# Sixteen weight blocks copied to a contiguous scratch tensor during the projection, and the scan's weight loads read from there

## The chip, the core and the metric

The kernel runs on one core of one Trainium2 chip. The metric is the device time of one execution in microseconds (us). Nothing runs beside it on the other cores. Five engines work in parallel, each through its own list of instructions, and meet at semaphores: PE multiplies matrices, ACT applies functions and copies, DVE and POOL do element-wise work, SP only issues transfers. ACT and POOL issue transfers too; those of SP appear in the profile as queue q1, those of ACT as q10, those of POOL as q0. The data move through 16 DMA engines, and the DMA share of a stretch is the mean busy share of these 16.

## The reference, cut to what matters

A layer over 2048 latent tokens with 256 context tokens in front. One input projection of the modulated, normalised tokens gives all branches; the columns of `in_w` are its outputs.

```
IN_SIZES = (M_WIDTH, M_WIDTH, M_WIDTH, M_WIDTH, M_WIDTH, N_GATE_COLS, P_WIDTH, P_WIDTH, N_BRANCH * D_MODEL)
names    = ('q',     'k',     'v',     'o',     'z_m',   'gates',     'p',     'z_p',   'g_branch')

parts_x = _split_proj((_rmsnorm(x, norm_w) * (1 + scale) + shift) @ in_w)
h_x     = _bi_mlstm(qx, kx, vx, lix, lfx, st_f, st_b)          # two scans over chunks of 128 tokens
y       = hn * sigmoid(parts['o']) * silu(parts['z_m'])        # then @ branch_m_w
y_p     = _pool_branch(parts_x, ...)                           # box means of p, times silu(z_p)
x       = x + gate * ((sigmoid(g_m) * y_m + sigmoid(g_p) * y_p) @ out_w)
return _rmsnorm(x, final_norm_w)
```

Here D_MODEL is 1024, there are 4 heads of 256, and `in_w` is 1024 rows by 8208 columns of float32. A row of it is thus 32,832 bytes long.

## The kernel before, in words

Everything is float32, multiplied as a high and a low part (three matmuls for each product), so every weight block is loaded raw, then split by ACT (`wh`) and DVE (`wl`). Four stages follow each other, each a block of its own at whose end all engines meet.

1. **Entry**, 0 to about 145 us: modulation, norms, and the transposed, split inputs `xlate`, `xtop`, `xctx` in on-chip memory.
2. **Projection**, about 145 to 908 us: the columns q, k, v and p with z_p ("s" in the code). The work is 32 units of 256 columns over 1024 tokens. A unit is seven block products M1, M6, M7, M5, M2, M4, M3 with sums of weight blocks and of results around them; an eighth product E belongs to the context tokens in eight of the units. That makes 232 positions, `POS`, and position p is about 3.3 us long. Every engine walks the same loop over p. ACT loads the next unit's raw weights (`raw_in`, in_w in pieces of 1 KB, or of 512 bytes for "s") when it splits M1. It splits three products ahead of PE. POOL makes the sums of weight blocks (`sums`, four for each unit) and the low parts of q and k (`low`). SP stores what is finished: q, k and v in transfers of 1 MB (`store_qk`, `store_v`), p and z_p in transfers of 256 KB. At the start of the second half of the tokens (from p = 113 on) seven blocks of inputs are rebuilt from a raw copy in HBM, `xr_d`, through a ring of eight slots called `stage` (`block_in`, L1058).
3. **Scan**, about 908 to 1940 us: PE interleaves the scan's steps with the projection's remaining columns: o, z, and the two gate parts g_m and g_p. Their weights are 16 blocks of 256 columns (`SCAN_COLS`, four for each of o, z, g_m, g_p). They are needed for both halves of the tokens, so 32 loads of 1 MB are made. ACT issues them (`pair`, L1772), one about every 31 us, into the buffer `wpair`, which is the same memory as `wraw`: the profile calls it `wraw`. The order is trip by trip: trip 0 takes the first block of o, z, g_m and g_p, trip 1 the second of each, and so on to trip 3; trips 4 to 7 repeat this for the other half of the tokens. The first of the 32 loads is issued at the end of stage 2 (L1144), the other 31 in stage 3. A load fetches, for each of the 128 partitions, eight pieces of 256 columns, which lie 128 rows of `in_w` apart.
   The scan's own data come through SP in many small transfers (`v_t`, `q_t`, `k_t`, `s_t`, `hother`), and its results go out the same way.
4. **Exit**, about 1940 to 2487 us: branch projections, merge, output projection, final norm.

The semaphores that the change touches: `prod_done` counts PE's products in stage 2, `pair_loaded` the loads of `wpair`.

Of the kernel before, what the change touches and what calls it, by code (L numbers as in the profile page):

```python
# [11 lines left out]
P = 128  # L12
D = 1024
KT = D // P
# [27 lines left out]
def f32(ap):  # L42

    return ap.bitcast(FP32)


def hybrid_block(nc, x, c, ctx, c_ctx, norm_w, ada_w, ada_b, in_w, gate_b, head_norm_w, pool_w,
# [5 lines left out]
    def scratch(name, shape):  # L53
        return nc.dram_tensor(name, shape, FP32, kind="Internal").ap()
# [17 lines left out]
    hsum_d = scratch("hsum_d", (NX, P, D))  # L72

    SCAN_COLS = [off + 2 * P * n for off in (O0, Z0, GM0, GP0) for n in range(KT // 2)]

    in_v = in_w[0].rearrange("(j p) n -> p j n", p=P)
    ada_v = ada_w[0].rearrange("(j p) n -> p j n", p=P)

    with ExitStack() as top:
        def sem(name):  # L80
            return top.enter_context(nc.semaphore(name))
# [45 lines left out]
        def sem2(name):  # L127
            done_with_2.append(nc.alloc_semaphore(name))
            return done_with_2[-1]
# [442 lines left out]
        wpair = wraw[:, :, :, :].rearrange("p a k f -> p (a k f)").rearrange("p (k f) -> p k f", k=KT)  # L572
        pair_loaded = sem("pair_loaded")
# [4 lines left out]
        with ExitStack() as ph:  # L578
# [44 lines left out]
            prod_done = sem2("prod_done")  # L623
# [8 lines left out]
            tm_stored = [sem2(f"tm_stored{n}") for n in range(NTM)]  # L632
            st_loaded = [sem2(f"st_loaded{n}") for n in range(NST // 2)]
            rb_hi = sem2("rb_hi"); rb_lo = sem2("rb_lo")
            xe_stored = sem2("xe_stored")


            UNITS = [(0, i, kind) for i in range(HEADS - 1) for kind in "qvsk"] + [(0, HEADS - 1, kind) for kind in "vkqs"]
# [40 lines left out]
            def is_qk(a):  # L679
                return kind_of(a) in "qk" and not is_ctx(a)  # L680
# [70 lines left out]
            def raw_block(u, d, n):  # L751

                return raw_of(u)[:, KH * d:KH * (d + 1), n * P:(n + 1) * P]
# [133 lines left out]
            @block.gpsimd  # L887
            def _(pool):

                nc.clear_and_free_semaphores(done_with)  # L890
                for part in range(2):
                    for (kh, tq), b in BLOCK_OF.items():
                        if b < 3:
                            pool.dma_start(xe_d[part, :, KH * kh:KH * (kh + 1), tq * TQ:(tq + 1) * TQ], f32(xlate[part][:, b])).then_inc(xe_stored, 16)

                def sums(u, n):

                    raw_need = 32 * (u // 2 + 1)
                    pool.wait_ge(raw_loaded[u % 2], raw_need)
                    if n == 1:  # L900
                        if u:
                            pool.wait_ge(op_lo, AT[u - 1, "M5"] + 1)
                        pool.tensor_tensor(ssum[:, 0], raw_block(u, 0, 1), raw_block(u, 1, 1), ALU.add).then_inc(s_made, 1)
                    elif n == 2:
                        if u:

                            pool.wait_ge(op_lo, AT[u - 1, "M6"] + 1)
                        pool.wait_ge(s_made, 4 * u + 1)
                        pool.tensor_tensor(ssum[:, 1], ssum[:, 0], raw_block(u, 0, 0), ALU.subtract).then_inc(s_made, 1)
                    elif n == 3:  # L910
                        if u:
                            pool.wait_ge(op_lo, AT[u - 1, "M7"] + 1)
                        pool.tensor_tensor(ssum[:, 2], raw_block(u, 0, 0), raw_block(u, 0, 1), ALU.subtract).then_inc(s_made, 1)
                    else:

                        pool.wait_ge(op_lo, AT[u, "M2"] + 1)
                        pool.wait_ge(s_made, 4 * u + 2)
                        pool.tensor_tensor(raw_block(u, 1, 0), raw_block(u, 1, 0), ssum[:, 1], ALU.subtract).then_inc(s_made, 1)

                def low(a):  # L920
                    e, tq = WHERE[PIECES[a][1]]
                    part = os[:, tq, :, e]
                    pool.wait_ge(qk_hi, nqk[a] + 1)
                    pool.tensor_tensor(part[:, :, 1, :], tmp[:, a % NTM].rearrange("p (c t) -> p c t", t=P),  # L924
                                       f32(part[:, :, 0, :]), ALU.subtract).then_inc(qk_lo, 1)

                for n in (1, 2, 3):
                    sums(0, n)
                for p in range(NSTEPS):
                    if p < NPOS:  # L930
                        u, name = POS[p]
                        if name == "M7":
                            sums(u, 4)
                            if u + 1 < NU:
                                sums(u + 1, 1)
                        if name == "M5" and u + 1 < NU:
                            sums(u + 1, 2)
                        if name == "M2" and u + 1 < NU:
                            sums(u + 1, 3)
                    for a in DUE[2].get(p, []):  # L940
                        if is_qk(a):
                            low(a)

            @block.tensor
            def _(pe):
# [467 lines left out]
        with ExitStack() as ph:  # L1413
# [350 lines left out]
            def _(act):  # L1764
# [7 lines left out]
                def pair(p):  # L1772
                    trip, kind, e = TILES[2 * p]

                    act.wait_ge(w_hi, W_BEFORE + 2 * p)
                    act.wait_ge(w_lo, W_BEFORE + 2 * p)
                    n = KINDS.index(kind) * (KT // 2) + trip % (NTRIP // 2)
                    act.dma_start(wpair, in_v[:, :, SCAN_COLS[n]:SCAN_COLS[n] + 2 * P]).then_inc(pair_loaded, 16)

                def split_hi(u):  # L1780
                    act.wait_ge(pair_loaded, 16 * (u // 2 + 1))
# [47 lines left out]
                for t in range(NSLOT):  # L1829
# [7 lines left out]
                    for p in range(1, NT // 2):  # L1837
                        if load_at[p] == t:
                            pair(p)
# [980 lines left out]
```

## Time and profile before

| | |
|---|---|
| median of 3 runs | 2487.7 us (2482.58 to 2488.55) |
| the profiled execution's own time | 2488.55 us |
| its span, first to last instruction | 2486.7 us |
| mean granted TensorE clock | 0.971 of full speed |
| PE busy | 2320.0 us, 93% |
| DVE, ACT, POOL busy | 58%, 38%, 23% |
| DMA, mean over the span | 195 GB/s |

The profiled execution took 1.85 us more than its span, and 0.85 us more than the median. PE is at 93% of the span, so the time goes where PE waits, and where its clock is granted at less than full speed. ACT, DVE and POOL have idle time on the whole, but they run only a few products ahead of PE, so that a long wait of one of them reaches PE.

### The profile page before, as it was taken

The numbers are of one execution on the slowest core, as the hardware profiler recorded it, in microseconds if no ns is written. First come the engines' busy times: TensorE is split into PE (matmuls) and PEld (weight loads), VectorE is DVE, ScalarE is ACT, GpSimd is POOL, SyncE is SP. The second block draws the span as 40 slices with busy tenths as digits, with TensorE's granted clock in tenths as the row PEclk, the third lists the DMA queues.
The fourth block names the chain that finished last, engine by engine and source line by source line (L and its number), as shares of the span: only waits on it lengthen the run. The fifth ranks groups of instructions, "written<-read, shape, count | busy, mean of one in ns | idle before, by whom it ended". The sixth has DMA issues, their size and how long they took to land. (4 is left out here: it accounts for less than half of the span.)

```text
span 2486.7 us, 35606 instructions
## 1 busy us (share of the span) xinstructions
PE 2320.0 (93%) x12515; PEld 1973.7 (79%) x12515; DVE 1453.3 (58%) x2655; ACT 954.8 (38%) x1938; POOL 575.4 (23%) x473
## 2 busy tenths in 40 slices
PE   6689999989899989999999999899999689999998
PEld 4668888866778868888888888788888578797978
DVE  1645555565556656566667656676666355656564
ACT  2633333343333323343434344434343435343532
POOL 0032433333334432121212111322120202121210
PEclk9789999989999999999999999999999799999999
DMA  9495755576557666888777787896777545656563
GB/s 287 148 263 117 160 135 143 159 209 132 98 140 147 186 223 193 228 240 214 215 244 216 225 298 225 230 212 204 222 218 228 187 155 186 212 188 208 190 205 108
DMA packets 428579, 484.90 MB, mean 195 GB/s; under 512 B 23752, under 2 KB 321268, under 8 KB 426868
## 3 DMA queue, kind: packets, MB, share of 16 engines
q1 hardware_dynamic: 345428, 388.24, 47.5%
q10 hardware_dynamic: 79616, 75.50, 18.7%
q0 software_dynamic: 3360, 18.88, 1.9%
q8 instruction: 103, 1.69, 0.3%
q14 instruction: 72, 0.59, 0.1%
HBM read 336.04 MB, written 146.49 MB: 194 GB/s over the span
## 5 line engine op out<-in xcount | busy, mean ns | idle before, releaser
L1735 PE MATMUL bank<-xlate,wh 128*128 128x512 f32 x2048 | 670.8, 401 | 15.5 <-DVE v_t L1869 10.5
L1735 PEld LDWEIGHTS bank<-xlate,wh 128*128 128x128 f32 x2048 | 373.2, 189 | 85.6 <-DVE v_t L1869 10.7
L1735 PE MATMUL bank<-xlate,wl 128*128 128x512 f32 x1024 | 409.8, 400 | 0.0
L1013 PE MATMUL bank<-xlate,wh 128*128 128x512 f32 x1024 | 330.4, 397 | 10.3 <-DVE wl L1213 9.8
L1013 PE MATMUL bank<-xtop,wh 128*128 128x512 f32 x768 | 251.6, 405 | 19.9 <-DVE wl L1213 10.9
L1013 PEld LDWEIGHTS bank<-xlate,wh 128*128 128x128 f32 x1024 | 190.9, 189 | 53.6 <-issue 12.2
L1735 PEld LDWEIGHTS bank<-xlate,wl 128*128 128x128 f32 x1024 | 193.6, 189 | 33.9
L1013 PE MATMUL bank<-xlate,wl 128*128 128x512 f32 x512 | 202.2, 395 | 0.0
L1228 DVE SCALAR_TENSOR_TENSOR tmp<-bank,psum 128x512 f32<-128x512 f32 x128 | 88.2, 689 | 177.8 <-PE bank L1013 106.9
L1013 PEld LDWEIGHTS bank<-xtop,wh 128*128 128x128 f32 x768 | 145.4, 194 | 52.3 <-ACT wh L1044 18.2
L1013 PE MATMUL bank<-xtop,wl 128*128 128x512 f32 x384 | 154.2, 402 | 0.0
L1892 DVE SCALAR_TENSOR_TENSOR state<-state,cols,bank 128x516 f32<-128x516 f32 x128 | 95.7, 748 | 100.0 <-PE bank L1696 99.7
L924 POOL TENSOR_TENSOR os<-tmp,os 128x512 fp32r<-128x512 f32 x64 | 94.0, 1470 | 127.6 <-ACT os L1152 127.3
L1709 PE MATMUL bank<-state_h,q_t 128*128 128x258 f32 x512 | 113.3, 284 | 9.6 <-DVE den L1949 9.6
L1044 ACT ACTIVATE wh<-ssum 128x512 fp32r<-128x512 f32 x96 | 60.3, 630 | 150.3 <-PE bank L1013 113.1
L1863 ACT ACTIVATE ysb<-bank 128x258 f32<-128x258 f32 x128 | 49.4, 386 | 178.5 <-PE bank L1696 177.9
L1897 DVE TENSOR_TENSOR wl<-wraw,wh 128x1024 fp32r<-128x1024 f32 x62 | 79.7, 1286 | 62.6 <-ACT wh L1783 62.5
L1013 PEld LDWEIGHTS bank<-xlate,wl 128*128 128x128 f32 x512 | 96.8, 189 | 21.4
L1696 PE MATMUL bank<-v_t,ek_h 128*128 128x258 f32 x576 | 110.6, 284 | 1.1 <-DVE ek_l L1874 1.1
L1709 PEld LDWEIGHTS bank<-state_h,q_t 128*128 128x128 f32 x512 | 87.5, 188 | 17.2 <-issue 7.9
L1922 DVE TENSOR_TENSOR p_l<-wexp,p_h 128x128 fp32r<-128x128 f32 x128 | 68.6, 536 | 54.3 <-ACT p_h L1804 54.3
L1213 DVE TENSOR_TENSOR wl<-ssum,wh 128x512 fp32r<-128x512 f32 x96 | 72.1, 751 | 45.7 <-ACT wh L1044 45.7
(304 smaller groups left out, 5271.0 us busy)
## 6 DMA issues: line engine op xcount, KB each, us to landing
v_t<-vk_d SPq DMA_DIRECT2D x144, 384.0 KB, 4.3
qk_d<-os SPq DMA_DIRECT2D x32, 1024.0 KB, 4.5
wraw<-in_in_w_dram ACTq DMA_DIRECT2D x32, 1024.0 KB, 12.7
q_t<-qk_d SPq DMA_DIRECT2D x128, 256.0 KB, 5.8
rawb<-in_in_w_dram ACTq DMA_DIRECT2D x32, 512.0 KB, 9.0
vk_d<-os SPq DMA_DIRECT2D x16, 1024.0 KB, 4.2
k_t<-qk_d SPq DMA_DIRECT2D x64, 256.0 KB, 6.2
wraw<-in_branch_m_w_dram SPq DMA_DIRECT2D x32, 512.0 KB, 3.8
```

The lines of the kernel that those rows point to most:

```text
L924: pool.tensor_tensor(part[:, :, 1, :], tmp[:, a % NTM].rearrange("p (c t) -> p c t", t=P), f32(part[:, :, 0, :]), ALU.subtract).then_inc(q ...
L1013: mm = pe.matmul(dst[:, :], a[:, kd, :], x_block(part, XB[name])[:, kd], start=(kd == 0 and n == 0), stop=(kd == KH - 1 and n == 2))
L1044: act.activation(op_ring(wh, p), op_source(u, name), ACT.Copy).then_inc(op_hi, 1)
L1213: dve.tensor_tensor(op_ring(wl, p), op_source(u, name), f32(op_ring(wh, p)), ALU.subtract).then_inc(op_lo, 1)
L1228: return dve.scalar_tensor_tensor(out=dst, in0=src[:, :], scalar=kscale(u), in1=in1, op0=ALU.mult, op1=ALU.add)
L1696: mm = pe.matmul(ubank[:, b, 0:VW], e_[:, L, b * P:(b + 1) * P], v_t[:, V, va, :], start=(n == 0), stop=(n == 2))
L1709: pe.matmul(XBANK[:, 0:VW], q_t[:, l % QS, b, qa, :], c_[:, L, b, :], start=(b == 0 and n == 0), stop=(b == HB - 1 and n == 2))
L1735: mm = pe.matmul(bank[m % 2][:, :], a[:, u % 2, k, :], xlate[part][:, BLOCK_OF[k // KH, tq], k % KH], start=(k == 0 and n == 0), stop=(k = ...
L1863: act.activation(ysb[:, :], YBANK[:, 0:VW], ACT.Copy).then_inc(y_read, 1)
L1892: dve.scalar_tensor_tensor(out=state[:, ch], in0=state[:, ch], scalar=col(d, NC + latent_chunk(l), 4, h), in1=upair[:, :, 0:VW], op0=ALU.m ...
L1897: dve.tensor_tensor(wl[:, u % 2], wpair[:, :, u % 2 * P:(u % 2 + 1) * P], f32(wh[:, u % 2]), ALU.subtract).then_inc(w_lo, 1)
L1922: dve.tensor_tensor(p_l[:, l % 2, :], wexp[:, l % 2, :], f32(p_h[:, l % 2, :]), ALU.subtract).then_inc(p_lo, 1)
```

## The change

A new tensor in HBM, `wpair_d`, has room for the 16 blocks of `SCAN_COLS`, each laid out as the buffer wants it: 128 rows of 8 KB without gaps. In stage 2 POOL gets 16 more transfers, each from HBM to HBM, at positions 20, 32, 44 and so on to 200. Copy n is made at position 20 + 12n, as the last thing that POOL does at that position, after a wait until PE has finished the product two before it (`prod_done` at least p - 1). Before stage 2 ends POOL waits until all 16 copies have landed. The 31 loads of stage 3 then read `wpair_d[n]` in place of `in_w`; the first load, L1144, still reads `in_w`.

```
@@ scratch tensors
     SCAN_COLS = [off + 2 * P * n for off in (O0, Z0, GM0, GP0) for n in range(KT // 2)]
+    wpair_d = scratch("wpair_d", (len(SCAN_COLS), P, KT, 2 * P))
@@ stage 2, semaphores
-            xe_stored = sem2("xe_stored")
+            pair_stored = sem2("pair_stored"); xe_stored = sem2("xe_stored")
@@ stage 2, POOL, inside and behind the loop over p
                         if is_qk(a):
                             low(a)
 
+                    for n, c0 in enumerate(SCAN_COLS):
+                        if p == 20 + 12 * n:
+                            pool.wait_ge(prod_done, p - 1)
+                            pool.dma_start(wpair_d[n], in_v[:, :, c0:c0 + 2 * P]).then_inc(pair_stored, 16)
+                pool.wait_ge(pair_stored, 16 * len(SCAN_COLS))
+
@@ stage 3, ACT, pair()
-                    act.dma_start(wpair, in_v[:, :, SCAN_COLS[n]:SCAN_COLS[n] + 2 * P]).then_inc(pair_loaded, 16)
+                    act.dma_start(wpair, wpair_d[n]).then_inc(pair_loaded, 16)
```

On POOL, in stage 2, around positions 113 to 128, before (`ssum` are the sums of weight blocks, `wraw` and `rawb` the raw weights of the even and the odd units, `os` the low parts of q and k):

```order
L903 TENSOR_TENSOR ssum<-wraw 128x512 [waits op_lo,raw_loaded0]
L924 TENSOR_TENSOR os<-tmp,os 128x4x128 [waits qk_hi]
L909 TENSOR_TENSOR ssum<-ssum,wraw 128x512 [waits s_made,op_lo,raw_loaded0]
L913 TENSOR_TENSOR ssum<-wraw 128x512 [waits op_lo,raw_loaded0]
L918 TENSOR_TENSOR wraw<-wraw,ssum 128x4x128 [waits s_made,op_lo,raw_loaded0]
L903 TENSOR_TENSOR ssum<-rawb 128x512 [waits op_lo,raw_loaded1]
L909 TENSOR_TENSOR ssum<-ssum,rawb 128x512 [waits s_made,op_lo,raw_loaded1]
L913 TENSOR_TENSOR ssum<-rawb 128x512 [waits op_lo,raw_loaded1]
L924 TENSOR_TENSOR os<-tmp,os 128x4x128 [waits qk_hi] x3
L918 TENSOR_TENSOR rawb<-rawb,ssum 128x4x128 [waits s_made,op_lo,raw_loaded1]
```

The same place with the change (the line numbers are one higher, since a line was added above):

```order
L904 TENSOR_TENSOR ssum<-wraw 128x512 [waits op_lo,raw_loaded0]
L925 TENSOR_TENSOR os<-tmp,os 128x4x128 [waits qk_hi]
L910 TENSOR_TENSOR ssum<-ssum,wraw 128x512 [waits s_made,op_lo,raw_loaded0]
L948 DMA wpair_d<-in_in_w_dram 1024x1x256 [waits prod_done]
L914 TENSOR_TENSOR ssum<-wraw 128x512 [waits op_lo,raw_loaded0]
L919 TENSOR_TENSOR wraw<-wraw,ssum 128x4x128 [waits s_made,op_lo,raw_loaded0]
L904 TENSOR_TENSOR ssum<-rawb 128x512 [waits op_lo,raw_loaded1]
L910 TENSOR_TENSOR ssum<-ssum,rawb 128x512 [waits s_made,op_lo,raw_loaded1]
L914 TENSOR_TENSOR ssum<-rawb 128x512 [waits op_lo,raw_loaded1]
L925 TENSOR_TENSOR os<-tmp,os 128x4x128 [waits qk_hi] x3
L948 DMA wpair_d<-in_in_w_dram 1024x1x256 [waits prod_done]
L919 TENSOR_TENSOR rawb<-rawb,ssum 128x4x128 [waits s_made,op_lo,raw_loaded1]
```

Two copies stand in this piece: copy 8 between the second and the third sum of a unit, copy 9 behind three low parts. Nothing else changes its place on POOL.

On ACT, in stage 3, at one of the weight loads, before:

```order
L1794 ACTIVATE wexp<-nm,cols 128x128
L1778 DMA wraw<-in_in_w_dram 128x8x256
L1800 ACTIVATE s_t<-bank 128x128
L1804 ACTIVATE p_h<-wexp 128x128
L1863 ACTIVATE ysb<-bank 128x258
```

And with the change:

```order
L1801 ACTIVATE wexp<-nm,cols 128x128
L1785 DMA wraw<-wpair_d 128x2048
L1807 ACTIVATE s_t<-bank 128x128
L1811 ACTIVATE p_h<-wexp 128x128
L1870 ACTIVATE ysb<-bank 128x258
```

The load keeps its place; 128 by 8 pieces of 256 elements have become 128 rows of 2048. The rows of PE, DVE and SP are the same as before.

## Rows read from the trace of the kernel before

**Rows 1.** Windows by stage, stages 2 and 3; the first line names the columns.
```profile
core 0: us, PE busy (x) PEld busy (x) DVE busy (x) ACT busy (x) POOL busy (x), PEclk, DMA share, GB/s
150.00:908.00 758.00, 727.20 (x3446) 595.26 (x3445) 428.38 (x610) 254.17 (x442) 275.68 (x193) 0.98 0.63 154
945.00:1940.00 995.00, 975.58 (x5352) 843.43 (x5350) 649.72 (x1452) 406.90 (x930) 203.96 (x209) 1.00 0.76 223
```
**Rows 2.** PE's waits in stage 3: 1015-1140, 1440-1475, then 1540-1665 us (total, times, longest).
```profile
PE bank L1686 <- DMA q_t<-qk_d: 4.1, 2, 2.2
...
PE bank L1709 <- DVE den L1949: 3.1, 2, 1.9
...
PE bank L1709 <- DVE den L1949: 6.4, 4, 2.5
PE bank L1735 <- issue: 1.5, 1, 1.5
```
**Rows 3.** Timeline of DVE in stage 3: start, us, line, and idle before it.
```profile
1594.53 0.48 DVE L1946 SCALAR_TENSOR_TENSOR num<-bank,cols,ysb 128x258 f32<-128x258 f32 x1 [5.99 <-DMA hsum_d<-num]
```
**Rows 4.** Windows of trips 1, 2 and 5 of stage 3, 120 us each.
```profile
1017.00:1137.00 120.00, 116.66 (x659) 101.06 (x657) 76.07 (x169) 49.18 (x118) 27.90 (x28) 1.00 0.89 215
1153.00:1273.00 120.00, 120.00 (x678) 104.57 (x677) 77.95 (x177) 48.99 (x118) 22.45 (x17) 1.00 0.73 223
1543.00:1663.00 120.00, 112.10 (x591) 94.84 (x590) 79.06 (x171) 46.09 (x103) 33.09 (x52) 1.00 0.85 200
```
**Rows 5.** DMA queues: 1017-1137, 1153-1273 (two rows), 1543-1663 us (packets, MB, share of 16 engines).
```profile
q10 hardware_dynamic: 4160, 4.19, 36.2%
...
q10 hardware_dynamic: 4160, 4.19, 15.5%
q0 software_dynamic: 144, 1.05, 2.1%
...
q10 hardware_dynamic: 4160, 4.19, 36.6%
```
**Rows 6.** PE's waits in stage 2: 484-570, then 570-605 us.
```profile
PE bank L1013 <- DVE wl L1213: 11.4, 4, 7.6
PE bank L1013 <- ACT wh L1044: 2.5, 1, 2.5
...
PE bank L1013 <- ACT wh L1044: 2.0, 1, 2.0
```
**Rows 7.** Timeline of POOL at the places of copies 8 and 9.
```profile
523.42 1.75 POOL L909 TENSOR_TENSOR ssum<-ssum,wraw 128x512 f32<-128x512 f32 x1
...
576.05 1.52 POOL L924 TENSOR_TENSOR os<-tmp,os 128x512 fp32r<-128x512 f32 x1 [0.19 <-ACT os L1152]
```
**Rows 8.** Timeline of ACT: a load's issue, and two waits for transfers.
```profile
531.18 6.27 ACTq L1062 DMA_DIRECT2D stage<-xr_d  x1
...
548.53 0.63 ACT L1190 ACTIVATE xlate<-stage 128x512 fp32r<-128x512 f32 x1 [8.79 <-DMA stage<-xr_d]
...
599.02 0.63 ACT L1154 ACTIVATE os<-tmp 128x512 f32<-128x512 f32 x1 [9.48 <-DMA qk_d<-os]
```
**Rows 9.** Windows in stage 2 around the two copies.
```profile
516.00:570.00 54.00, 39.72 (x145) 30.20 (x144) 37.62 (x48) 24.27 (x44) 15.52 (x10) 0.84 0.67 175
529.00:537.00 8.00, 7.23 (x31) 5.31 (x29) 6.84 (x12) 2.31 (x4) 0.00 (x0) 1.00 0.96 187
537.00:547.00 10.00, 4.58 (x12) 3.32 (x12) 1.99 (x3) 2.19 (x4) 0.00 (x0) 0.80 0.89 130
583.00:599.00 16.00, 16.00 (x71) 12.80 (x69) 5.71 (x8) 1.48 (x3) 5.51 (x4) 1.00 0.89 215
```
**Rows 10.** POOL's issue of six 1 MB transfers in pieces (ns min/median/max).
```profile
L894 POOL DMA_DIRECT2D xe_d<-xlate x6: 752/754/911, 146.1 to 150.0; - x6
```
**Rows 11.** Waits of POOL and of ACT in stage 2, 200-900 us (total, times, longest).
```profile
POOL wraw L918 <- DVE wl L1213: 187.9, 15, 33.4
...
ACT os L1152 <- DMA vk_d<-os: 4.1, 3, 1.5
```

## The prediction

> **What bounds the kernel now.** I read the windows by stage first. In both stages that the change touches PE is busy for nearly all of the time: 727.2 of 758 us in the projection and 975.6 of 995 us in the scan [rows 1]. So no engine's work can be taken off PE here; all that the change can move is the 31 us of PE's idle time in the one stage and the 19 us in the other, and the clock that goes with them. The DMA share is 0.63 and 0.76 there: high, but a mean, and the question is at which moments it is full.
>
> Then I read PE's waits in the scan, stretch by stretch. In 1015 to 1140 us they are 4.1 us, for `q_t` to land; in 1540 to 1665 us they are 6.4 and 1.5 us; around 1450 us there are 3.1 us [rows 2]. The 6.4 us name DVE, but DVE itself had been waiting 5.99 us for a store of the scan's results [rows 3], so these too are transfers that come late. Between these stretches PE never waits. The windows say what sets them apart: the two stretches with waits are the trips 1 and 5, with DMA shares of 0.89 and 0.85, and trip 2, just as long and with the same work, has 0.73 and a PE that is 100% busy [rows 4]. The queues say why. ACT's queue moves the same four weight loads in each of these stretches, 4.19 MB, but they take 36.2% and 36.6% of the 16 DMA engines in trips 1 and 5, and 15.5% in trip 2 [rows 5]. Over 120 us and four loads that is 0.362 x 120 / 4 = 10.9 us of all the DMA engines for a load in trips 1 and 5, and 0.155 x 120 / 4 = 4.65 us in trip 2. Trips 1 and 5 read the same columns, the second block of each of o, z, g_m and g_p: those columns are slow to read, whenever it is done.
>
> In the projection PE waits 13.9 us between 484 and 570 us and 2.0 us between 570 and 605 [rows 6]. Two of these end on a transfer: ACT stood still 8.79 us for a `stage` block until 548.5 us, and 9.48 us for a store of q until 599.0 us [rows 8]. The second cost PE 2.0 us, so ACT can lose about 9.5 - 2.0 = 7.5 us before PE notices.
>
> **Loads in the scan (removed cost).** A contiguous load of 1 MB in 8 KB rows stands in trip 2's stretch, as POOL's load of `p_d`: 2.1% of 120 us, which is 2.5 us [rows 5]. So each load gives back 10.9 - 2.5 = 8.4 us of the DMA engines in trips 1 and 5 and 4.65 - 2.5 = 2.15 us elsewhere. The share in trip 1 falls from 0.89 to 0.89 - 4 x 8.4 / 120 = 0.61, below that of trip 2, where nobody waits. I therefore take all of the waits in trips 1 and 5 as gone, 4.1 + 6.4 + 1.5 = 12.0 us, and 0.5 of the 3.1 us around 1450 us, where SP's own reloads fill the engines. Together -12.5 us, and at most 12.0 + 3.1 = -15.1. The clock was granted at 1.00 in all these trips [rows 4], so nothing comes back there. The other 23 loads hide behind a busy PE before and after: 0. The lower bound is a gain of 0, if the waits have another cause.
>
> **Copies in the projection (added cost).** POOL's issue: six transfers of 1 MB in pieces took 0.754 us each to issue [rows 10]; the copy has twice the pieces, so 0.75 to 1.5 us, 16 times, 12 to 24 us of POOL. POOL waits 187.9 us for DVE at one line alone [rows 11]. The new wait for `prod_done` asks for a product that is two positions old: where POOL runs ahead of it, the next thing on POOL is a wait for DVE that ends later still. What is queued behind is the next sum or low part, which ACT and PE want several us later. I take 0, with 2 us as the upper bound.
>
> The transfers themselves: no row shows one from HBM to HBM. From below a copy costs the DMA engines the 2.5 us of 8 KB rows; as a read of these columns 4.65 us, and 10.9 us for the four copies of slow columns (copies 1, 5, 9 and 13); from above read and write add up, 4.65 + 2.5 = 7.2 and 10.9 + 2.5 = 13.4 us. I take 5 and 10.9 us, nearest to the same read into on-chip memory. What this is worth depends on whether the engines have a gap at that moment.
>
> Copy 8 is issued when POOL has made the second sum, at 525.2 us [rows 7], and finds the DMA engines full: 0.96 until 537 us and 0.89 until 547 us [rows 9], most of it the ACT queue, whose last load had stuck in its issue for 6.27 us and is the one that ACT waits for until 548.5 us [rows 8]. The wait already reaches PE, so all of the copy does: +5 us (2.5 to 7.2).
>
> Copy 9 is issued behind a low part that ends at 577.6 us [rows 7], is slow, and the engines are at 0.89 from 583 to 599 us [rows 9], when the store that ACT waits for lands. The wait is already past what PE forgives. A part of the copy is through before that store is issued, so I take 7.5 of its 10.9 us: +7.5 (4 to 13.4).
>
> The other 14 copies: at ACT's stops for stores of v the waits are short, 1.5 us at most [rows 11], and with 5 us more they stay below the 7.5 us that PE forgives. The three slow ones, copies 1, 5 and 13, could pass it by 10.9 - 7.5 = 3.4 us each. I take 1 us for all (0 to 10).
>
> The clock: from 516 to 570 us it was granted at 0.84 on the mean, with its lower level (1.2 GHz) in the middle of PE's wait [rows 9], so (1 - 0.84) x 54 = 8.6 us of full speed went with about 14 us of waiting, part of it while PE stood still anyway. For 12.5 us more of waiting I take +3 (0 to 8).
>
> The rule that speaks against this change is in the Trainium skill, "DMA: Bandwidth & Descriptors", section "Issuing engines are not separate DMA queues": transfers of all issuing engines run on the same 16 DMA engines and interleave. By that rule POOL's copies take room from ACT's and SP's transfers, as above; without it copies 8 and 9 would cost nothing and the sum would be -12.5 us. In the trace ACT's queue takes what SP's leaves, which agrees.
>
> **The sum.** -12.5 + 5 + 7.5 + 1 + 3 = +4 us on the profiled execution's 2488.55 (span 2486.7 and 1.85 around it), which is 2492.5. That execution was 0.85 us above the median of the runs, so against the median I say 2492.
>
> **The rivals.**
> *The copies find room (A).* POOL's copies reach into gaps, or delay only what nobody waits for. For it: the mean share is only 0.63 [rows 1], and the copies of units elsewhere do find gaps. Against it: the engines are full at copies 8 and 9. Then only the scan's gain is left, and up to 3 us of cost: 2488.5 - 12.5 = 2476, at best 2473.5.
> *The copies are dear (B), slower.* Reading and writing HBM in one transfer costs 7.2 us and 13.4 us, or more when two queues read slow columns at once. The place is the wait for `stage` at 548 us and the store at 599 us: +7.2 + 13.4, the slow copies 1, 5 and 13 pass the 7.5 us by 5.9 each, of which half reaches PE, +9, and the clock +8: 37.6 - 12.5 = +25, so 2514. It decides as soon as a copy takes over 7.5 us of the engines in the normal columns.
> *The layout gives nothing in the scan (C).* The waits in trips 1 and 5 stay, because they come from SP's many small transfers; the cost of 16.5 us stays too: 2505. Against it are the loads of trip 2, equal in all but their columns.
> The Trainium skill, same page, section "Specifications", gives 512 bytes as the smallest piece for full rate; by that rule pieces of 1 KB lose nothing against 8 KB. The trace disagrees already in the normal columns, 4.65 us against 2.5, and nothing in that rule knows slow columns.
>
> **How the numbers follow.** I give the forecast 0.50, A 0.18, B 0.17, C 0.15. The forecast's own range is 2480 to 2505. This kernel's runs tell a change from none at about 0.3%, 7.5 us. Faster by more: 0.16 from A and 0.04 from the forecast's lower end, 0.20. Slower by more: 0.16 from B, 0.10 from C, 0.09 from the forecast's upper end, 0.35. Between: 0.45. For the range I leave out the outer halves of A and B: 2474 to 2510.
>
> **What would show it.** Right: in trips 1 and 5 a DMA share near 0.61 and PE without waits; ACT's q10 at about 8% of such a stretch; the loads land several us sooner. ACT's waits for `stage` near 548 us and for q's store near 599 us longer by 5 and about 7 us, PE's with them, and a clock below 0.84 in that stretch. POOL's sums no later than now where no transfer is late. Wrong, A: PE's waits between 516 and 605 us as before. Wrong, B: q0 in the projection above 16 x 7 us of all engines, and new waits of PE near copies 1, 5 and 13. Wrong, C: trips 1 and 5 keep their waits though q10's share falls.

## The result and the profile after

| | before | after |
|---|---|---|
| median of 4 runs, same chip | 2488.12 us (2482.58 to 2494.43) | 2548.86 us (2544.98 to 2551.54) |
| ratio, 95% interval | | 1.0242 (1.0213 to 1.0270) |
| span of the profiled execution | 2486.7 us | 2545.3 us |
| end of the projection (first matmul of the scan) | 918.8 us | 989.6 us |
| length of the scan (to its last matmul) | 1018.2 us | 1005.3 us |
| rest (exit) | 549.7 us | 550.3 us |

The change makes the kernel 60.7 us slower. I had said 2492 with 2474 to 2510, and 0.45 for no difference: wrong. The time lies beyond every rival's too (2476, 2514, 2505). The scan won 12.9 us on the profiled executions, nearly the 12.5 forecast; the projection lost 70.8 where 16.5 had been forecast.

The windows of the scan answer to [rows 1, 4]. The first fence is the whole scan of before, the second the whole scan of after and then the trips 1, 2 and 5 in it. The same loads are issued 73, 68 and 68 us later there (trip 1's first at 1090.5 us in place of 1017.5), so the stretches are moved with them.

```profile
919.00:1937.00 1018.00, 998.22 (x5456) 862.30 (x5457) 656.66 (x1465) 413.60 (x941) 210.28 (x220) 1.00 0.77 226
```

```profile
core 0: us, PE busy (x) PEld busy (x) DVE busy (x) ACT busy (x) POOL busy (x), PEclk, DMA share, GB/s
990.00:1995.00 1005.00, 997.70 (x5457) 864.24 (x5457) 653.59 (x1465) 414.96 (x941) 207.34 (x220) 1.00 0.69 229
1088.00:1208.00 120.00, 120.00 (x684) 104.85 (x683) 79.51 (x175) 50.77 (x121) 28.63 (x30) 1.00 0.70 237
1220.00:1340.00 120.00, 120.00 (x681) 104.69 (x680) 79.31 (x178) 49.51 (x119) 22.41 (x17) 1.00 0.67 219
1611.00:1731.00 120.00, 120.00 (x648) 103.89 (x648) 86.08 (x193) 51.60 (x114) 32.34 (x53) 1.00 0.69 230
```

The loads themselves, all 31 on their line (ns of an issue, then us from issue to landing; 10.0/12.8/17.7 before):

```profile
L1785 ACTq DMA_DIRECT2D wraw<-wpair_d x31: 326/327/366, 995.6 to 1941.3; - x31
...
DMA to landing us min/median/max: 5.4/6.7/11.0
```

ACT's queue in trip 1 and in trip 5, then the two longest of PE's waits that are left in the whole scan:

```profile
q10 hardware_dynamic: 576, 4.19, 9.0%
...
q10 hardware_dynamic: 576, 4.19, 9.5%
...
PE bank L1742 <- DVE wl L1904: 2.9, 1, 2.9
PE bank L1716 <- DVE den L1956: 2.2, 2, 1.4
```

Four loads in trip 5 take 9.5% of the engines where they took 36.6% [rows 5]: 0.095 x 120 / 4 = 2.9 us each against 10.9, and in trip 1 it is 2.7 us. The DMA share falls from 0.89 to 0.70 in trip 1 and from 0.85 to 0.69 in trip 5, and PE is busy for all 120 us of both. So the waits of these trips, for `q_t` and behind `hsum_d` [rows 2, 3], are gone. The 2.9 us left stand before the first weight loads and were there before too. Over the whole scan PE stands still 7.3 us where it was 19.7.

In the projection the loss splits cleanly. The same window of before, from 150 us to the end of the projection, stands first, and that of after in the second fence.

```profile
150.00:918.80 768.80, 727.53 (x3447) 595.36 (x3445) 430.58 (x614) 254.17 (x442) 277.67 (x193) 0.97 0.63 156
```

```profile
150.00:989.60 839.60, 738.12 (x3436) 602.51 (x3434) 436.65 (x614) 253.52 (x442) 287.50 (x209) 0.94 0.69 162
```

PE was idle 768.8 - 727.5 = 41.3 us and is now 839.6 - 738.1 = 101.5 us: +60.2. The other +10.6 us is PE's busy time for the same products, at a granted clock of 0.94 against 0.97.

What the copies did to the engines is in the group of their line: issue time, POOL's waits before it, landing.

```profile
L948 POOL DMA_DIRECT2D wpair_d<-in_in_w_dram x16: 816/839/862, 213.9 to 871.7; - x16
its engine sat idle before it (us, times) until:
  PE bank L1020: 11.7, 5
...
DMA to landing us min/median/max: 11.1/16.4/21.5
```

Added up over their packets, the 16 copies took 119.0 us of all 16 DMA engines: 3.2 to 8.7 us each for the twelve normal ones, and 13.7, 10.9, 12.6 and 11.1 us for copies 1, 5, 9 and 13, those of the columns that read slowly.

Copy 1 shows how the loss arises. Queues of after, first 264-276 us, when copy 1 (issued at 259.39) is under way and ACT's raw load (issued at 263.4 and 263.8) is pending, with that load's landing time; then 291-303 us, when that queue's next load is under way and a store of q and copy 2 are pending; last 278-286 us, between the two.

```profile
q0 software_dynamic: 203, 0.83, 95.5%
q1 hardware_dynamic: 129, 0.13, 3.1%
q10 hardware_dynamic: 7, 0.00, 0.1%
...
wraw<-in_in_w_dram ACTq DMA_DIRECT2D x1, 512.0 KB, 25.9
...
q10 hardware_dynamic: 1002, 1.00, 97.2%
...
qk_d<-os SPq DMA_DIRECT2D x1, 1024.0 KB, 19.1
...
q10 hardware_dynamic: 1665, 0.84, 48.1%
q1 hardware_dynamic: 838, 1.33, 44.1%
```

In the first two stretches the engines are not shared: the transfer of slow columns that came first has 95.5 or 97.2% of them, and the others get what is left until it is through. It isn't always so. From 278 to 286 us, with copy 1 done, ACT's raw load and SP's stores have nearly equal shares. What decides between the two is not shown. Timelines of POOL, ACT and PE over the same stretch (start, us, line, idle before it and its releaser), and in a second fence the windows of 303-315 and 315-318 us:

```profile
259.39 0.84 POOL L948 DMA_DIRECT2D wpair_d<-in_in_w_dram  x1
...
289.75 1.30 POOL L904 TENSOR_TENSOR ssum<-wraw 128x512 f32<-128x512 f32 x1 [11.65 <-DMA wraw<-in_in_w_dram]
291.01 1.74 POOL L925 TENSOR_TENSOR os<-tmp,os 128x512 fp32r<-128x512 f32 x1
...
289.79 0.93 ACTq L1062 DMA_DIRECT2D rawb<-in_in_w_dram  x2
...
312.03 0.60 ACT L1175 ACTIVATE os<-bank 128x512 fp32r<-128x512 f32 x1 [17.31 <-DMA qk_d<-os]
...
315.10 1.09 PE L966 MATMUL bank<-ident,tmp 128*128 128x128 f32 x4 [18.53 <-DVE os L1390]
```

```profile
303.00:315.00 12.00, 0.00 (x0) 0.00 (x0) 1.34 (x3) 2.61 (x5) 0.00 (x0) 0.50 0.57 171
315.00:318.00 3.00, 2.90 (x9) 2.55 (x10) 1.75 (x3) 0.60 (x1) 0.00 (x0) 0.50 0.00 0
```

Read it as a chain. Copy 1 holds the engines, so the raw load behind it lands 25.9 us after its issue, at 289.7; the same load took 12.0 us before the change. The delay of 13.9 us is about the 13.7 us that the copy took. POOL's first sum (L904) had waited for it 11.65 us, and the low part of q (L925), which stands behind that sum on POOL, is ready only at 292.7. SP then issues the store of q, 9 us later than before the change (292.82 against 283.86). But ACT's next raw load, a slow one, has been issued at 289.79 and has the engines until 303, and from then on copy 2, issued at 295.19, takes its part of them beside the store. The store lands at 312, ACT stood still for 17.31 us, and PE for 18.53, where it had no wait at all before. Copy 2 has a share in this: in the run "4 slow" below, which has copy 1 without it, the same wait of PE is 13.03 us. While PE stands still its clock goes to 0.50 of full speed, the lower level (1.2 GHz), and it is still 0.50 in the first 3 us of matmuls behind the stop. I put the 10.6 us of slower matmuls down to such stops; they were not added up one by one.

### The profile page after: what moved, and what is told of

Same layout as the page of the kernel before. It is cut to its first block and busy times, and to the rows that moved or that the text cites. A ratio compares the mean times of both kernels' runs of the same rounds, so it can differ in the third digit from the quotient of the medians.

```text
span 2545.3 us, 35623 instructions
## 1 busy us (share of the span) xinstructions
PE 2329.1 (92%) x12515; PEld 1981.9 (78%) x12515; DVE 1457.5 (57%) x2655; ACT 955.9 (38%) x1938; POOL 582.6 (23%) x489
## 5 line engine op out<-in xcount | busy, mean ns | idle before, releaser
L1742 PEld LDWEIGHTS bank<-xlate,wh 128*128 128x128 f32 x2048 | 373.9, 189 | 83.3 <-DVE v_t L1876 10.7
L1220 DVE TENSOR_TENSOR wl<-ssum,wh 128x512 fp32r<-128x512 f32 x96 | 75.2, 783 | 97.3 <-ACT wh L1051 97.2
L925 POOL TENSOR_TENSOR os<-tmp,os 128x512 fp32r<-128x512 f32 x64 | 95.3, 1494 | 137.0 <-ACT os L1159 136.7
L1051 ACT ACTIVATE wh<-ssum 128x512 fp32r<-128x512 f32 x96 | 60.2, 630 | 139.7 <-PE bank L1020 86.1
L1703 PEld LDWEIGHTS bank<-v_t,ek_h 128*128 128x128 f32 x576 | 90.5, 190 | 3.5 <-issue 2.3
```

Of the source, the lines that this page charges most:

```text
L1051: act.activation(op_ring(wh, p), op_source(u, name), ACT.Copy).then_inc(op_hi, 1)
L1220: dve.tensor_tensor(op_ring(wl, p), op_source(u, name), f32(op_ring(wh, p)), ALU.subtract).then_inc(op_lo, 1)
L1703: mm = pe.matmul(ubank[:, b, 0:VW], e_[:, L, b * P:(b + 1) * P], v_t[:, V, va, :], start=(n == 0), stop=(n == 2))
L1742: mm = pe.matmul(bank[m % 2][:, :], a[:, u % 2, k, :], xlate[part][:, BLOCK_OF[k // KH, tq], k % KH], start=(k == 0 and n == 0), stop=(k = ...
```

## The experiments

"Projection" and "scan" are the stretches of the table above; before has 918.8 and 1018.2 us. All ratios are against runs of the kernel before on the same chip (its medians 2488.1 to 2493.1). The two stretches come from one profiled execution of each kernel. Those of in eighths, source x, ACT issues, and 4 slow, spread were 6 to 10 us faster than the median of their kernel, that of 4 slow, ahead 7 us slower; a cost read off two profiles is good to some 10 us, and the ratios decide.

| kernel | ratio (95% interval) | projection ends | scan | copies' engine time |
|---|---|---|---|---|
| after | 1.0242 (1.0213, 1.0270) | 989.6 | 1005.3 | 119.0 us |
| copies only | 1.0310 (1.0259, 1.0361) | 990.2 | 1026.5 | 116.5 |
| loads only | 0.9922 (0.9892, 0.9952) | 920.0 | 1005.3 | 0 |
| waits only | 1.0008 (0.9989, 1.0027) | 916.0 | 1027.1 | 0 |
| in eighths | 1.0044 (1.0026, 1.0062) | 938.8 | 1008.3 | 90.4 |
| 12 normal | 1.0105 (1.0087, 1.0122) | 942.1 | 1020.6 | 66.7 |
| 4 slow | 1.0092 (1.0077, 1.0107) | 961.4 | 1003.1 | 48.2 |
| source x | 1.0029 (1.0013, 1.0045) | 936.1 | 1004.5 | 48.3 |
| ACT issues | 1.0120 (1.0096, 1.0144) | 962.9 | 1003.0 | |
| 4 slow, ahead | 1.0072 (1.0047, 1.0097) | 958.6 | 1007.0 | 52.5 |
| 4 slow, behind | 1.0049 (1.0032, 1.0067) | 951.9 | 1005.9 | 38.4 |
| 4 slow, spread | 0.9948 (0.9932, 0.9964) | 916.0 | 1003.4 | 23.7 |

### Copies only: the loads read `in_w` as before

```
-                    act.dma_start(wpair, wpair_d[n])...
+                    act.dma_start(wpair, in_v[:, :, SCAN_COLS[n]:SCAN_COLS[n] + 2 * P])...
```

> The copies are made as in the changed kernel, but the scan loads its weights from in_w as before. Theory T (the 1 MB copies occupy the DMA engines in the projection, and transfers that the projection needs stand behind them): the whole loss stays and the scan's gain goes, the changed kernel's 2549 us plus 12 to 13 us, about 2561. Rival L (the loads from the new layout also cost something, and the scan's gain is not real): 2549 or below.

Measured: 2569.13 us against 2490.09, 8 us above what was expected. The projection ends at 990.2 us, as in after; the scan takes 1026.5 us.

### Loads only: no copies, the loads read 8 KB rows of another tensor

```
-                            pool.dma_start(wpair_d[n], in_v[:, :, c0:c0 + 2 * P])...
-                    act.dma_start(wpair, wpair_d[n])...
+                    act.dma_start(wpair, xr_d[n % 8].rearrange("k p t -> (k p t)").rearrange("(p k f) -> p k f", p=P, k=KT))...
```

> No copies; the 31 scan loads read 1 MB blocks of 8 KB rows from another scratch tensor (the raw inputs), so the weights of o, z and the gates are other numbers. This is the scan's half of the change alone. Theory T: 12 to 13 us below the kernel before, about 2475.5, with PE free of waits in trips 1 and 5. Rival L: no gain, 2488.

Measured: 2473.64 us. The two halves of the change are separate: the copies cost the projection all it loses (70.8 us in after, 1.2 without them), and contiguous loads give the scan what it wins. In the ratio they are worth 0.0078 x 2490 = 19 us (12 to 27), more than the 12.9 between the two profiled executions, though the interval holds that too. The windows of the whole scan say why: first those of copies only, then of loads only.

```profile
990.00:2017.00 1027.00, 1005.92 (x5458) 868.06 (x5459) 654.80 (x1467) 413.73 (x941) 209.44 (x220) 0.99 0.76 224
```

```profile
920.00:1925.00 1005.00, 997.28 (x5455) 864.29 (x5456) 654.62 (x1465) 414.27 (x941) 206.23 (x220) 1.00 0.69 229
```

PE's idle time differs by 21.1 - 7.7 = 13.4 us, the forecast's waits. The rest, 8.6 us, is the same matmuls at a lower clock. With the old loads everywhere the scan ran at 0.99 in two of three profiles (copies only and waits only, PE busy for 1005.9 and 1006.3 us), and in the profile of before at 1.00, with 998.2. With new loads it isn't fixed either: PE was busy for 994.6 us in 4 slow and for 1001.0, at 0.99, in eighths. So the clock may add some us to what the loads give back; how many, these single profiles don't settle.

### Waits only: POOL waits for the product, but copies nothing

```
                             pool.wait_ge(prod_done, p - 1)
-                            pool.dma_start(wpair_d[n], in_v[:, :, c0:c0 + 2 * P])...
```

(and the old loads in the scan)

> POOL waits for prod_done at the same 16 positions, but issues no copy, and the scan loads from in_w. Theory T: the wait costs nothing, 2488 plus or minus 3. Rival W (POOL, held back by the new waits, makes its sums and low parts late, and this is the loss): most of the 60 us, 2530 or more.

Measured: 2493.27 us, no difference. POOL's new wait and its place cost nothing that the runs can tell; it is the transfers.

### In eighths: the same copies, each in eight parts at eight positions in a row

The wait at the end of stage 2 counts the parts; that line is not shown, here and below.

```
-                        if p == 20 + 12 * n:
+                        if p - (20 + 12 * n) in range(8):
+                            s = p - (20 + 12 * n)
-                            pool.dma_start(wpair_d[n], in_v[:, :, c0:c0 + 2 * P])...
+                            pool.dma_start(wpair_d[n, 16 * s:16 * (s + 1)], in_v[16 * s:16 * (s + 1), :, c0:c0 + 2 * P])...
```

> Each copy is cut in eight parts of 16 rows (128 KB), one at each of eight positions in a row, so 128 small copies with the same bytes and the same pieces. Theory T in the form that a copy blocks the engines for as long as it lasts (a burst): the longest block falls from about 11 us to 1.4 us, and most of the loss goes: 2480 to 2495. Rival C (only the sum of the engines' time counts, 16 copies of 5 to 13 us): no change, about 2549.

Measured: 2503.23 us, above the 2480 to 2495 expected and far below the rival's 2549. The 128 parts, and PE's waits to the end of the projection:

```profile
L949 POOL DMA_DIRECT2D wpair_d<-in_in_w_dram x128: 522/522/557, 213.5 to 853.8; - x128
...
DMA to landing us min/median/max: 2.8/6.1/16.9
```

```profile
PE bank L1021 <- DVE wl L1221: 26.2, 6, 8.0
PE bank L1021 <- ACT wh L1052: 14.8, 2, 9.8
```

The same bytes from the same columns cost the projection 938.8 - 918.8 = 20.0 us in place of 70.8, though POOL issues eight times as often. In ratios, against loads only, it is 0.012 in place of 0.032: 30 us against 80. So what costs is above all how long one transfer holds the engines, not how many bytes there are. The parts also take less of the engines in sum, 90.4 us in place of 119.0, but that is a quarter less, and the loss in the projection falls by more than half by either count.

### The twelve normal blocks alone, and the blocks 1, 5, 9 and 13 alone

```
-                        if p == 20 + 12 * n:
+                        if p == 20 + 12 * n and n % 4 != 1:      # "12 normal";  == 1 in "4 slow"
-                    act.dma_start(wpair, wpair_d[n])...
+                    act.dma_start(wpair, wpair_d[n] if n % 4 != 1 else in_v[:, :, SCAN_COLS[n]:SCAN_COLS[n] + 2 * P])...
```

> Only the 12 copies of the normal columns are made, at their places, whole; the loads of the four slow blocks read in_w as before. Theory T with slow blocks as the main cause (the four copies that hold the engines for 11 to 14 us): most of the projection's 70 us goes, 15 to 30 us stay, and the scan gains 1 to 3 us: 2500 to 2515. Rival C (each of the 16 copies costs the same): 12/16 of 70 us stay, 2540.

> Only copies 1, 5, 9 and 13, those of the slow blocks, whole and at their places; the other loads read in_w. Theory T with slow blocks as the main cause: 40 to 50 us of the projection's 70, less 12 in the scan: 2518 to 2528. Rival C: 4/16 of 70 us, less 12: 2493. The two parts together need not make 70 us, since one late transfer can hide behind another.

Measured: 2517.28 us, 2 us above its range, and 2516.83 us, 1 us below. In the projection the twelve cost 942.1 - 918.8 = 23.3 us (1.9 each) and the four 961.4 - 918.8 = 42.6 us (10.7 each). Together that is 65.9 of 70.8: the costs nearly add. In the scan the four give everything, 1003.1 us, and the twelve nothing that stands out: 1020.6 us, where the profiles with the old loads have 1018.2 to 1027.1. PE's wait behind copy 1, in "4 slow":

```profile
312.16 1.09 PE L966 MATMUL bank<-ident,tmp 128*128 128x128 f32 x4 [13.03 <-DVE os L1390]
```

### Source x: copies of the same shape out of another tensor

```
+                            x_v = x[n // 4 % 2 * D:n // 4 % 2 * D + D, :].rearrange("(j p) n -> p j n", p=P)
-                            pool.dma_start(wpair_d[n], in_v[:, :, c0:c0 + 2 * P])...
+                            pool.dma_start(wpair_d[n], x_v[:, :, n % 4 * 2 * P:(n % 4 + 1) * 2 * P])...
```

> All 16 copies at their places, with the same shape (1024 pieces of 1 KB), but out of the input x, whose rows lie 4096 bytes apart; so the scan's o, z and gate weights are other numbers. Theory T: a copy without slow columns holds the engines for 3 to 6 us, and the loss falls to that of the normal copies, 2490 to 2515. Rival H (a transfer from HBM to HBM is dear in itself, whatever it reads): 2549, as the changed kernel.

Measured: 2499.51 us; the projection loses 17.3 us. The landing times:

```profile
L949 POOL DMA_DIRECT2D wpair_d<-in_x_dram x16: 816/836/859, 216.0 to 823.0; - x16
...
DMA to landing us min/median/max: 6.0/10.3/17.3
```

Pieces of 1 KB out of rows of 4096 bytes make copies of 48.3 / 16 = 3.0 us of the engines; out of `in_w`, with its rows of 32,832 bytes, they take 7.4. So a copy within HBM is not dear as such, and neither are pieces of 1 KB: contiguous loads took 2.7 to 2.9 us. `in_w` is the dear part, its second column blocks above all. These copies cost the projection nearly as much as the parts in eighths, 17.3 against 20.0 us, with about half of their engine time, so the sum alone doesn't set the cost.

### ACT issues the copies, right behind its raw loads

```
                             raw_in(u + 1)
+                            for n, c0 in enumerate(SCAN_COLS):
+                                if u == POS[20 + 12 * n][0]:
+                                    act.dma_start(wpair_d[n], in_v[:, :, c0:c0 + 2 * P]).then_inc(pair_stored, 16)
```

(and none on POOL; ACT waits for all of them at the end of stage 2)

> The 16 copies are issued by ACT, each right behind the load of the next unit's raw weights, in the same units as before; POOL issues none. Theory P (what costs most is that a copy gets ahead of a raw load, POOL then stands at its sum and its low parts and the stores behind them come late): the raw loads are first on their queue, and the loss is halved at least, 2500 to 2520. Rival Q (it does not matter which transfer is held up, since the engines are full): 2540 to 2560.

Measured: 2524.88 us, between the two ranges, the projection +44.1; the loss is less, but not halved. Behind a raw load on one queue the copy comes second, and PE's waits from 240 to 540 us become small (4.9 and 1.4 us at 281 and 400). The stores behind the copies are still late: in the second half PE waits 8.3, 13.5, 9.0 and 6.9 us at 610, 677, 729 and 781.

### The four slow blocks at other places, ahead of and behind the raw load

```
-                    for n, c0 in enumerate(SCAN_COLS):
-                        if p == 20 + 12 * n:
+                    for m, u in enumerate((3, 5, 8, 11)):
+                        c0 = SCAN_COLS[4 * m + 1]
+                        if p == AT[u, "M1"] - 5:      # "ahead";  - 1 in "behind"
```

> Only the four slow blocks are copied, whole, by POOL, all in the first half of the projection, in units 3, 5, 8 and 11, at two positions (about 6 us) ahead of the issue of the next raw weight load; the other loads read in_w. Theory P (a copy that gets ahead of a raw load makes POOL's sum, its low parts and the store behind them late): PE loses 5 to 18 us at two or more of the four places, 15 to 40 us in all, less 15 us in the scan: 2490 to 2515. Rival Q (in this half the engines have gaps, and the place in the unit does not matter): the same as the next run.

> The same four copies in the same units, but two positions (about 6 us) behind the issue of the raw weight load. Theory P: the raw load is on the engines first, the copy ends before the next one, and the projection loses at most 8 us; with 15 us back in the scan 2473 to 2483, below the kernel before. Rival Q: the same as the run before.

Measured: 2511.72 us, within its range, and 2504.83 us, far above the 2473 to 2483 expected; +39.8 and +33.1 us in the projection. PE's waits from 150 to 945 us, ahead and then, in the second fence, behind:

```profile
PE bank L1021 <- ACT wh L1052: 31.0, 6, 11.8
PE bank L1021 <- DVE wl L1221: 16.3, 3, 9.6
PE bank L967 <- DVE os L1391: 16.2, 2, 12.6
```

```profile
PE bank L1021 <- DVE wl L1221: 38.3, 6, 11.0
PE bank L1021 <- ACT wh L1052: 18.0, 4, 8.8
```

The place matters little. Behind the raw load the waits for q's store (L967) are down to 0.9 us, but others come: in "behind" DVE stood still 19.09 us for a `tmp` buffer whose store of z_p landed at 243.9 us, as the copy did, and PE then 11.0 us. My idea that a copy behind the raw load would be free has fallen. At all the places tried here a hold of 7 to 14 us met some transfer that was wanted sooner.

### The four slow blocks in 32 parts, three positions apart

```
-                    for n, c0 in enumerate(SCAN_COLS):
-                        if p == 20 + 12 * n:
+                    for m in range(32):
+                        n, s = 4 * (m // 8) + 1, m % 8
+                        c0 = SCAN_COLS[n]
+                        if p == 14 + 3 * m:
-                            pool.dma_start(wpair_d[n], in_v[:, :, c0:c0 + 2 * P])...
+                            pool.dma_start(wpair_d[n, 16 * s:16 * (s + 1)], in_v[16 * s:16 * (s + 1), :, c0:c0 + 2 * P])...
```

> The four slow blocks, each in eight parts of 128 KB, the 32 parts at every third position from 14 to 107; so no part holds the engines for more than about 1.5 us. If the length of a single hold decides: the projection loses 0 to 3 us, the scan gains 15, 2473 to 2477, below the kernel before. If the sum of the engines' time decides: a loss of the size of the run before or more.

Measured over 10 runs: 2479.20 us against 2492.22, ratio 0.9948 (0.9932 to 0.9964); that is 2 us above the 2473 to 2477 expected. It beats both kernels. Its projection, then its parts:

```profile
150.00:916.00 766.00, 725.74 (x3445) 594.08 (x3443) 437.31 (x614) 253.80 (x442) 292.21 (x226) 0.98 0.66 162
```

```profile
L950 POOL DMA_DIRECT2D wpair_d<-in_in_w_dram x32: 524/524/557, 198.5 to 492.8; - x32
...
DMA to landing us min/median/max: 3.1/5.1/11.1
```

PE's idle time in the projection is 40.3 us, that of before is 41.3; in this profile nothing is lost, and the scan has all of the gain (1003.4 us). The ratio is 0.0026 above that of loads only, 6.5 us, but the two intervals meet, so a small cost isn't excluded. POOL waits 56.5 us at its copies (48.8 for PE's products and 7.7 for DVE), five times as long as in after, and PE's waits are none the longer. The four blocks took 48.2 us of the engines as whole copies and take 23.7 as parts. No run spreads them over more time without making them shorter, so how much the shorter hold does and how much the smaller sum is not separated here.

## Why the prediction was wrong, step by step

**The bound and the loads of the scan: right, a little small.** Waits of 12.5 us were to go and 12.4 went (19.7 to 7.3 us). A load takes 2.7 to 2.9 us of the engines where 2.5 was said, the landing fell to 6.7 us, and the four slow blocks alone carry the gain, as their rows had said [rows 5]. Trip 1 has a DMA share of 0.70 where 0.61 was forecast: the loads gave back what was said (36.2 to 9.0%), but the forecast held the other queues fixed, and SP's went from 47.8 to 53.9% in the same 120 us. "Nothing comes back there" on the clock is not safe: one profile at 1.00 [rows 4] did not show that other executions of the old loads run at 0.99. The price of pieces was misread: 4.65 us against 2.5 was laid to pieces of 1 KB, but the copies of source x have pieces of 1 KB too and took 3.0 us, so the size of the piece alone is not what costs.

**POOL's issue and waits: right.** 0.84 us an issue was within 0.75 to 1.5, the waits 11.7 us, the cost 0 (waits only).

**The transfers' size: right in sum.** 12 x 5 + 4 x 10.9 = 104 us was assumed, 119.0 measured, 7.4 on the mean.

**Copies 8 and 9: right in the size.** In after, copy 8 is issued at 557.06 and copy 9 at 613.28. ACT's wait for `stage`, 8.79 us in [rows 8], has become two, and q's store is waited for 13.31 us instead of 9.48:

```profile
571.90 0.63 ACT L1197 ACTIVATE xtop<-stage 128x512 fp32r<-128x512 f32 x1 [6.47 <-DMA stage<-xr_d]
...
583.39 0.63 ACT L1197 ACTIVATE xlate<-stage 128x512 fp32r<-128x512 f32 x1 [6.02 <-DMA stage<-xr_d]
...
639.19 0.63 ACT L1161 ACTIVATE os<-tmp 128x512 f32<-128x512 f32 x1 [13.31 <-DMA qk_d<-os]
...
610.00:635.00 25.00, 25.00 (x110) 20.20 (x108) 10.41 (x14) 5.33 (x9) 9.85 (x8) 1.00 1.00 133
```

The engines are full for 25 us around copy 9. PE's waits between the second sum before copy 8 and the end of copy 9's shadow are 26.2 us (2.60, 7.60, 4.87, 0.61, 4.34 and 6.14); the same products had 15.3 (2.47, 7.60, 3.28 and 1.97). That is +10.9 us where +12.5 was forecast.

**"The other 14 copies: I take 1 us for all (0 to 10)": this step failed.** PE's waits elsewhere in the projection rose from 13.8 to 63.8 us, +50. The waits behind the three slow copies 1, 5 and 13 are 34.9 of it, 18.53, 5.65 and 10.71 us, the first with copy 2's help. The last two, as DVE's waits and PE's:

```profile
447.09 0.69 DVE L1235 SCALAR_TENSOR_TENSOR tmp<-bank,psum 128x512 f32<-128x512 f32 x1 [14.74 <-issue]
...
800.13 0.69 DVE L1235 SCALAR_TENSOR_TENSOR tmp<-bank,psum 128x512 f32<-128x512 f32 x1 [18.31 <-issue]
...
801.52 1.19 PE L1020 MATMUL bank<-xlate,wh 128*128 128x512 f32 x2 [10.71 <-DVE wl L1220]
...
DMA to landing us min/median/max: 2.2/2.6/18.2
```

DVE waits there for a `tmp` buffer. The profile names no releaser, but a store of z_p (L819, last row: 2.6 us on the median, 18.2 at worst) had stood behind the copy and landed just before DVE went on, at 447.01 and at 800.05 us. The reasoning had two faults. It looked for copies that meet an existing wait, with full engines [rows 6, 9], and judged the rest by ACT's short waits for stores of v alone [rows 11]; the raw loads that POOL waits for, the stores of q and DVE's stores of p and z_p were left out. And it took 7.5 us as what PE forgives everywhere, from one wait of ACT for one store [rows 8]. But the raw load behind copy 1 was late by the copy's whole length (13.9 us against 13.7), since the copy had the engines nearly to itself, and a late raw load delays a low part on POOL, that a store, and that store can fall behind the next raw load. A copy of 13.7 us so became 18.5 us of PE's time, 13.0 with no copy 2 behind it. The copies in eighths show that the long holds are the main cause: the same bytes, the same columns, nearly the same moments, and 50.8 of 70.8 us are gone (50 of 80 in ratios).

**The clock: direction right, size off.** +3 was said, +10.6 us of slower matmuls came, with 60 us of new waits and not 12.5. For each us of waiting that is less than was said.

**The rivals.** A, copies find room, is refuted for copies of 1 MB; it is true of copies 1, 5, 9 and 13 in parts. B, the dear copies, was the nearest: new waits at copies 1, 5 and 13, as it named. The sign given for it, above 16 x 7 = 112 us for all copies, held with 119.0. Its deciding point did not: normal copies took (119.0 - 48.3) / 12 = 5.9 us on the mean, and only two of the twelve 7.5 or more. And its 37.6 us of cost are half of what came: it priced the slow copies by what they exceed 7.5 us, and let half of that reach PE. C is refuted by loads only. The Trainium skill, "DMA: Bandwidth & Descriptors", section "Issuing engines are not separate DMA queues", says that transfers of all issuing engines interleave. The trace agrees that they compete, and from 278 to 286 us two queues do have 48.1 and 44.1%. But from 264 to 276 us one had 95.5%, and another with a load pending 0.1%. I had reckoned with a fair loss of room throughout; beside a long hold there was none to share.

**What stays open.** Why the second block of each group of columns reads slowly isn't settled. Nor is it shown which of the normal copies causes which of the smaller waits (15.1 us in sum); only their total of 23.3 us when they are alone. What decides whether two queues share the engines or one holds them is open too, and so is how the shorter hold and the smaller sum divide the gain of the parts.

## What to carry to other kernels

Price a background transfer by how long it holds the DMA engines at a stretch, not by its bytes over the mean idle share, and try it in short parts: here the four blocks in parts of 128 KB, three products apart, cost the projection nothing that its profile shows, where whole they cost 42.6 us. Before moving all of a set, find which members carry the gain; here four of sixteen blocks carried it, and the other twelve cost more than they gave. A slack read off one wait holds for that wait alone; a late transfer must be followed through the queue of every engine that waits for it.

## What the runs showed of the hardware

- One queue can have nearly all of the DMA engines: 95.5% for 12 us (copy 1) and 97.2% for 12 us (a raw load of slow columns) while others had transfers pending. A 512 KB load issued 4.4 us after copy 1 landed after 25.9 us, 12.0 before the change. At other moments two queues share, 48.1 and 44.1% from 278 to 286 us.
- The second block of 256 columns of each of o, z, g_m and g_p in `in_w` reads slowly: from ACT's share in trips 1, 5 and 2 [rows 5], 170 and 172 ns of an engine for a piece of 1 KB against 73, and 42 to 45 ns for a KB of contiguous rows. The raw loads of that block of q, k and v land after 13.4 to 16.1 us, those of other blocks of them after 7.8 to 12.2.
- A copy in 16-row parts takes less of the engines than the same copy whole: 90.4 against 119.0 us for all blocks, 23.7 against 48.2 us for the blocks 1, 5, 9 and 13.
- POOL needs 0.84 us to issue a copy of 1024 pieces and 0.52 us for one of 128.
- The granted clock stays at 0.50 for the first 3 us of matmuls behind a stop of 18.5 us (315 to 318 us in after).
